# Every fourth row's dot product: a product on GpSimd and a sum on ScalarE in place of one operation on VectorE

## The reference

```python
eidx = jnp.take_along_axis(cidx, pos, axis=-1)      # 8 heads x 16 experts for each token
g = jax.nn.softmax(top_s, axis=-1)
u_sel = jnp.take(u, eidx, axis=0)                   # rows of 1024 numbers
a = jax.nn.gelu(jnp.einsum('chkd,cd->chk', u_sel, xc), approximate=False)
w = (g * a).astype(x.dtype)
v_sel = jnp.take(v, eidx, axis=0)
return jnp.einsum('chk,chkd->cd', w, v_sel)
```

## Time and profile before

| | |
|---|---|
| median of 3 runs | 2847.54 us (2843.93 to 2849.05) |
| the profiled execution | 2847.81 us, its span 2846.0 us |
| PE busy | 2144.6 us (75%) |
| DVE busy | 1585.1 us (56%) |
| ACT busy | 832.7 us (29%) |
| POOL busy | 749.6 us (26%) |
| all dot products (L1551) | 479.5 us in ring buffers, 158.3 us in arena buffers, x512 |
| all gathers issued (L2705) | x384 and x128, 545.30 MB with the queue's other transfers |

### The profile page before, as it was taken

The page is one execution under the profiler, slowest core; times in us unless marked ns, Lnnn a source line. Parts: engine busy times, 40 slices in busy tenths (PEclk is TensorE's granted clock), DMA queues, the critical chain, the costliest instruction groups (busy, mean ns, idle before and its releaser), DMA issues.

```text
span 2846.0 us, 33622 instructions
## 1 busy us (share of the span) xinstructions
PE 2144.6 (75%) x11828; PEld 1079.6 (38%) x11828; DVE 1585.1 (56%) x3312; ACT 832.7 (29%) x2340; POOL 749.6 (26%) x675
## 2 busy tenths in 40 slices
PE   6886767767567683776666667598987878988897
PEld 3552332222012262343332223276875443333332
DVE  5268648578446528856889877646555242222222
ACT  2215333433333312433343444323221111111111
POOL 1113434334335012334454445211111000000000
PEclk9888877778669786888998898899998889999999
DMA  7588999989999615899999899802111369999994
GB/s 274 213 339 314 408 422 405 422 339 393 422 421 412 239 67 212 327 422 406 416 396 397 329 421 415 359 33 88 58 45 63 119 281 415 420 420 419 417 419 186
DMA packets 122690, 894.55 MB, mean 314 GB/s; under 512 B 16400, under 2 KB 16912, under 8 KB 21776
## 3 DMA queue, kind: packets, MB, share of 16 engines
q0 software_dynamic: 77760, 545.30, 47.1%
q1 hardware_dynamic: 44752, 347.01, 30.1%
HBM read 893.82 MB, written 4.72 MB: 316 GB/s over the span
## 4 chain that ended last, share of the span: by engine, by line
PE 40%; DVE 27%; DMA 24%; ACT 4%; issue 3%; POOL 1%; SPq 0%; DVEq 0%; PEldq 0%; ACTq 0%; POOLq 0%
PE ps L155 39%; DMA ring<-in_peer_uv,idx_u 15%; DVE ring L1551 7%; DVE arena L76 5%; DMA ring<-in_w_gu 4%; ACT arena L125 3%; DMA arena<-in_peer_uv,idx_u 2%; DVE arena L1551 2%; DVE iu L113 2%; DVE arena L109 2%; PE ps L158 1%; DVE arena L97 1%; DVE small L93 1%; DMA arena<-in_w_gu 1%; DVE arena L118 1%
## 5 line engine op out<-in xcount | busy, mean ns | idle before, releaser
L155 PE MATMUL ps<-ring,arena 64*64 64x512 f32 (+3 forms) x4512 | 843.6, 715 | 339.4 <-ACT arena L125 293.0
L155 PE MATMUL ps<-arena 128*128 128x128 f32 (+8 forms) x3496 | 653.1, 501 | 196.8 <-ACT arena L125 160.3
L1551 DVE CUSTOM_DVE_ANT_0 ring<-ring,h 128x1024 f32<-128x1024 f32 x384 | 479.5, 1249 | 258.4 <-DMA ring<-in_peer_uv,idx_u 223.6
L2705 POOL DMA_INDIRECT ring<-in_peer_uv,idx_u x384 | 428.9, 1117 | 516.7 <-PE ps L155 477.3
L155 PEld LDWEIGHTS ps<-ring,arena 64*64 64x64 f32 (+3 forms) x4512 | 211.3, 149 | 841.3 <-ACT arena L125 578.1
L125 ACT ACTIVATE arena<-arena 128x1 f32<-128x1 f32 (+2 forms) x1051 | 270.8, 258 | 841.6 <-DVE arena L1551 739.7
L155 PEld LDWEIGHTS ps<-arena 128*128 128x128 f32 (+4 forms) x3496 | 323.3, 175 | 480.2 <-ACT arena L125 273.9
L125 ACT ACTIVATE arena<-ps 128x512 f32<-128x512 f32 (+2 forms) x222 | 122.7, 553 | 773.4 <-PE ps L155 702.5
L76 DVE TENSOR_TENSOR arena<-arena,ps 128x512 f32<-128x512 f32 (+1 forms) x154 | 90.9, 591 | 391.4 <-ACT arena L125 312.2
L155 PE MATMUL ps<-ring,hT 128*128 128x512 f32 (+2 forms) x832 | 281.2, 496 | 4.7 <-ACT hT L125 2.4
L2705 POOL DMA_INDIRECT arena<-in_peer_uv,idx_u x128 | 145.4, 1136 | 335.3 <-PE ps L155 259.5
(11 more groups left out here) (128 smaller groups left out, 1509.8 us busy)
## 6 DMA issues: line engine op xcount, KB each, us to landing
ring<-in_w_gu SPq DMA_DIRECT2D x98, 1024.0 KB, 22.5
ring<-in_w_down SPq DMA_DIRECT2D x52, 1024.0 KB, 22.6
ring<-in_peer_wq SPq DMA_DIRECT2D x16, 2048.0 KB, 11.3
arena<-in_w_gu SPq DMA_DIRECT2D x30, 1024.0 KB, 22.3
ring<-in_w_in SPq DMA_DIRECT2D x10, 2048.0 KB, 18.5
ring<-in_w_mod SPq DMA_DIRECT2D x16, 1024.0 KB, 7.3
arena<-in_w_in SPq DMA_DIRECT2D x6, 2048.0 KB, 11.8
ring<-in_w_o SPq DMA_DIRECT2D x6, 2048.0 KB, 8.2
```

The source lines that it names most:

```text
L155: return self.e.matmul(o, lhsT, rhs, start=start, stop=stop, skip_group_check=True)
L1551: v.done(v.e.tensor_tensor_reduce(out=row, in0=row, in1=h[:, n // 128, :], scale=1.0, scalar=0.0, op0=ALU.mult, op1=ALU.add, accum_out=aa[ ...
L2705: g.e.indirect_dma_start(out=landing(l, n), out_offset=None, in_=d["peer_uv"], in_offset=bass.IndirectOffsetOnAxis(ap=idx_u[:, n:n + 1], a ...
```

## The change

For the rows 3, 7, 11 to 255 of each layer VectorE skips `dots(n)`. GpSimd multiplies the row in place with `h`, after it has issued the gather six rows ahead. ScalarE then copies the product onto itself with an accumulated sum into the column of `aa`, before the gelu. All other rows stay as they were.

```diff
+DOTS_ASIDE, ASIDE_AT = range(3, 256, 4), 6
...
                 for n in range(256):
-                    dots(n)
+                    if n not in DOTS_ASIDE:
+                        dots(n)
...
                     w = aa[:, n:n + 1]
-                    a.wait_ge(*at("dots", l, n))
+                    if n in DOTS_ASIDE:
+                        row = landing(l, n)[:, 0:D]
+                        a.wait_ge(*at("product", l, n))
+                        a.act(row, row, ACT.Copy, accum_out=w)
+                    else:
+                        a.wait_ge(*at("dots", l, n))
                     a.act(w, w, ACT.Gelu)
...
-                for n in range(256 + 5):
+                def product(n):
+
+                    row = landing(l, n)[:, 0:D]
+                    g.wait_ge(*at("landed", l, n))
+                    g.tt(row, row, h[:, n // 128, :], ALU.mult, ("product", l, n))
+
+                for n in range(256 + ASIDE_AT):
                     if n < 256:
                         gather(n)
+                    if n - ASIDE_AT in DOTS_ASIDE:
+                        product(n - ASIDE_AT)
```

## The result

The changed kernel took 3112.93 us (median of 4 runs, 3107.73 to 3117.53) against 2848.3 us before on the same chip: ratio 1.0925, interval 1.0911 to 1.0939. That is 264.6 us slower. The direction was forecast, but the time lies 204 us above the forecast 2909 us and 128 us above the upper end of the range, 2985 us. The profiled execution has a span of 3108.3 us.

What follows compares the result with a forecast made beforehand. Row arrival by DMA was taken to bound the gather stages mostly, VectorE only in parts. Terms 20 + 26 - 18 + 37 - 9 + 5 = 61 us on 2847.81 us gave about 2909 us, range 2852 to 2985 us.

Steps and rivals of the forecast that it cites:

- The ring: Through GpSimd's queue, ScalarE and TensorE: a four-row cycle can't be shorter than 5.9 + 3W us.
- W: TensorE's weighted sum of one row, interpolated from the granted clock at 1.23 to 1.54 us.
- Rival D: Few rows in buffers, so products wait for landing and no loop forms; 2852 us, chance 0.11 shared with B.
- B: Rival: buffers and slack absorb the latency, the port takes back VectorE's saving; 2852 us, chance 0.11 with Rival D.
- Its fixed part: Gather, product, hand-over, ScalarE's sum and small operations, release to GpSimd: 5.88 us per four-row cycle, without weighted sums.
- So half is exposed: TensorE's other work, 0.9 to 4.2 us a cycle: half hidden before the moved row, half lengthening the cycle.
- Which cycles pay: Settled stretches: plus 20 and 26 us; mixed ones: plus 37 where DMA holds, minus 9 where VectorE does.
- the queue's slack: About 9 us by which gathers may issue late in each of two settled stretches, credited as minus 18 us.
- VectorE's relief: 128 dot products removed, 168 us of work, on the path only where VectorE is the limit.
- rival A: VectorE is the limit wherever the DMA share is below 1, so faster: about 2803 us, chance 0.10.
- rival C: At the VectorE-GpSimd port products nearly always get in first, VectorE losing 2.25 us for 1.31 saved: 2958 us, chance 0.15.
- Ends: Last row of each layer, with nothing behind to hide it: 1.31 us becomes 3.6, plus 5 us together.

Runs made afterwards that it cites:

- e1: Changed kernel with GpSimd's product five gathers ahead in its queue instead of six: 2918.17 us, ratio 1.0231.
- e9: Changed kernel with GpSimd zero fills in place of the product, still six gathers ahead, ScalarE still waiting and summing: 3102.09 us, ratio 1.0888.
- e6: Changed kernel with the 29 background pieces of the second chunk's attention moved away from the rows behind the product: 3074.30 us, ratio 1.0793.
- e10: Changed kernel with GpSimd zero fills in place of the product, four gathers ahead instead of six: 2849.37 us, ratio 1.0001.
- e3: Changed kernel with every fourth row's product on VectorE instead of GpSimd, the sum still on ScalarE: 2865.09 us, ratio 1.0052.
- e5: Kernel before, all dot products on VectorE, plus three GpSimd zero fills per used row that no other engine needs: 2877.07 us, ratio 1.0102.
- e4: Kernel before, all dot products on VectorE, plus GpSimd products whose output is not used: 2948.22 us, ratio 1.0349.

## Why the prediction was right in direction and wrong in size

**The ring: right.** "A cycle can't be shorter than 5.9 + 3W" was the mechanism. e1 shows it (one place is worth 1.52 us a cycle) and e9 shows that it is nearly all of the loss. Rival D is refuted by the 11.9 us that the products waited for their rows, and B by the time.

**Its fixed part: right.** The sum of gather, product, hand-over, ScalarE's part and the 0.31 was 5.88 us, 6.38 with the 0.5 us added for port and background; measured 1.12 + 2.42 + 0.20 + 2.23 + 0.31 = 6.28. The product was put at 2.25 and took 2.35 (median) to 2.42 us (mean); twice the 512-column row, 2.54, and the carried-on step, 2.03, held it between them.

**W: mis-sized.** I took it from the mean granted clock of a stretch, 1.41 us on average. By the eight matmuls of each row, W of the rows moved is 1.77 us (1.32 before), of the next two 1.61 and 1.34: 4.7 instead of 4.2 us a cycle. TensorE is kept from its next weighted sum for 4.6 us on average before row r (5.29 us idle below), and 74% of these rows then take over 1.8 us, near the 1.98 us at 1.2 GHz; before it was 23%.

**"So half is exposed": the step that failed.** Besides fixed part and W the cycle has 13.69 - 6.28 - 4.7 = 2.7 us; the prediction had 1.15 (half of TensorE's other busy time over the cycles). That is 1.5 of the 1.9 us by which its cycle of 11.8 us was short; W is 0.5. Taken from the start and end of every weighted sum, the 2.7 us are these: 1.9 us between the weighted sums of r, r + 1 and r + 2; 0.6 in front of gather r + 10, which starts that much later than the 0.31 us behind its weighted sum; and 0.1 in front of row r's. In the gaps between these weighted sums TensorE works on pieces for 1.7 us a cycle and is idle for 0.5 (where there is no gap the records overlap a little, so the net is 1.9).

So about half of TensorE's other work was exposed, as assumed. But this work was 3.1 us a cycle and not 2.3. Measured row by row it was 2.9 in the kernel before already: I had subtracted an interpolated 4W from the busy time of a stretch, and the rest came out too small. And neither TensorE's idle time inside the exposed pieces nor the late gather had a term. A usual place, timeline of 228 to 262 us:

```profile
235.77 1.99 PE L155 MATMUL ps<-ring,arena 64*64 64x512 f32 x8 [0.26 <-ACT arena L125]
...
237.69 2.19 PE L158 MATMUL ps<-cst,arena 128*128 128x128 f32 x16
...
239.81 1.95 PE L155 MATMUL ps<-arena 64*64 64x512 f32 x16
```

The weighted sum of r + 1 starts 4.0 us after row r's, and TensorE's own piece (L158) fills the 2 us between them. In 12 of 126 cycles TensorE is idle for over 2 us in these gaps. One of the dearest, timeline of 1928 to 1941 us, lines of other work left out:

```profile
1929.13 2.65 POOL L134 TENSOR_TENSOR ring<-ring,h 128x1024 f32<-128x1024 f32 x1
...
1934.01 1.98 PE L155 MATMUL ps<-ring,arena 64*64 64x512 f32 x8 [5.29 <-ACT arena L125]
1934.03 1.28 ACT L125 ACT_TABLE_LOAD   x1
1935.33 0.63 ACT L125 ACTIVATE arena<-arena 128x512 f32<-128x512 f32 x1
...
1935.99 1.57 ACT L125 ACTIVATE ring<-ps,small 128x128 f32<-128x128 f32 x4
...
1938.41 1.28 ACT L125 ACT_TABLE_LOAD   x1
...
1939.70 0.53 ACT L125 ACTIVATE arena<-arena 128x1 f32<-128x1 f32 x2
...
1940.72 1.98 PE L155 MATMUL ps<-arena 64*64 64x512 f32 x8 [4.73 <-ACT arena L125]
```

The dot product of row r + 1 had been done since 1929.6 us, yet its weighted sum starts 6.7 us after row r's: ScalarE does 5.7 us of background, two table loads in it, before it comes to r + 1, and TensorE stands idle 4.73 us. Gather r + 9 and product r + 4 come as much later. e6 moved pieces to where row r is waited for anyway and got 39 us back. The cycles without pieces on TensorE, rows 174 to 221 of the first layer, have a mean of 11.50 us, and 11.5 was forecast for that stretch; that is luck, since W was 0.9 us a cycle too short there and the exposed work, of which there was none, 0.5 too long. The same rows of the second layer, with pieces, took 12.86 us against 11.1.

**Which cycles pay: wrong, but the number did not come from it.** Floor and chain were compared with VectorE as the limit of half the mixed cycles (term -9) and the queue's slack as a one-time credit (-18). The ring holds in every stretch (the DMA share is at most 0.90), and a loss that returns each cycle uses 9 us of slack up within a few. But with the prediction's own chain in every stretch in which it is longer than the cycle before, the sum is 29 x 0.2 + 20.6 x 1.0 + 27.1 x 0.1 + 22 x 1.2 = 55 us, and its terms 20 + 26 - 18 + 37 - 9 gave 56. The miss is the length of the cycle: 13.47 us by the spans of the gathers against 11.8, over 127.5 cycles about 210 us, near the missing 204. One reading of the floor was off as well: the sixth stretch comes to 9.65 us and not 9.9; no term of the sum uses it.

**VectorE's relief: no net gain.** 168 us of dot products went away. The forecast was that VectorE's busy time falls, by less than that; it was 1586.4 us, against 1585.1 before. 119 us came back as blocked time of the other dot products: 384 x 1.245 = 478 us became 398.5 + 198.9 = 597. The other 50 came back in VectorE's remaining work, 35 of them in its TENSOR_TENSOR and SCALAR_TENSOR_TENSOR operations; the 58 of the form arena<-arena,small 128x512 took 0.89 us instead of 0.72. Where nothing is blocked (e10, VectorE busy for 1442.2 us) the kernel isn't faster either. The times refute rival A's 2803 us. That VectorE, at 85% in 1290 to 1600 us, set no part of the time there is not shown: e10 also has ScalarE's 1.25 us of latency, which cost 16 us in e3, and GpSimd's time in front of the gathers, which cost up to 28 us in e5, so a gain of that order could be hidden in it. One hint is that rows 62 to 90, where VectorE has the searches, took 166 us in e10's trace instead of 172 over both layers; single executions differ by more than these 6 us.

**The port, rival C: real, but not at its price here.** Each product blocks VectorE for 0.93 us on average, and it costs 12 to about 20 us inside the ring, where VectorE's time lies beside it, 39 once the ring is opened and about 71 with all dot products on VectorE (e4). By the Trainium skill ("SBUF — State Buffer", Who interferes with whom) it is GpSimd's reading of SBUF that contends; e4 and e5, where a product and a fill differ by 1.2 us of blocked VectorE for each, agree.

**Ends: right.** 3.6 us were expected from the start of the last product of a layer to the end of its sum. At the end of the first layer:

```profile
1054.21 2.35 POOL L134 TENSOR_TENSOR ring<-ring,h 128x1024 f32<-128x1024 f32 x1 [3.54 <-DMA ring<-in_peer_uv,idx_u]
...
1056.60 1.06 ACT L125 ACTIVATE ring<-ring 128x1024 f32<-128x1024 f32 x1 [0.55 <-POOL ring L134]
...
1057.78 0.53 ACT L125 ACTIVATE arena<-arena 128x1 f32<-128x1 f32 x2
```

1057.78 - 1054.21 = 3.57 us, against the 1.31 us of a dot product and its read the earlier trace rows, which ended the layer before.

**The range.** Its upper end let W rise on 60 cycles only, and had no case in which the pieces count with their waits. An upper bound with all of TensorE's other work exposed, 2.3 us more on the mean cycle instead of 1.15, would have been wider.

## What to carry to other kernels

An operation that is put into an in-order queue behind a transfer that waits for a buffer closes a ring through everything that frees the buffer. Write the ring down, count how many rows of it run in parallel, and charge its length to every turn: with background work between its steps that work counts in full, with its own waits, and every place earlier in the queue takes one step out. Before work is moved off an engine that looks busy, ask whether its relief shows in the end at all; here the same relief with the ring opened and the port left alone (e10), less what the new path itself costs, changed the time by 0.01%.

## What was not expected of the hardware

- A dot product whose record has begun is stretched by a GpSimd product that starts after it. Timeline of the changed kernel:

```profile
1041.06 3.78 DVE L1552 CUSTOM_DVE_ANT_0 ring<-ring,h 128x1024 f32<-128x1024 f32 x1
...
1041.39 2.35 POOL L134 TENSOR_TENSOR ring<-ring,h 128x1024 f32<-128x1024 f32 x1
```

The dot product starts 0.33 us earlier by its record, lasts 3.78 us instead of 1.23, and ends 1.1 us after the product, which took its usual 2.35 us. Nine more dot products of this trace, with records that begin 0.2 to 0.45 us before a product's, do the same (3.65 to 3.91 us). In the earlier trace rows the one that started second waited. Whether it had really begun, or its record starts before its first access, the trace doesn't say.

- A gather right behind a product took 1.49 us on GpSimd on average, over 1.5 us in 73 of 124 cases (2.03 at 821.02 above); the other gathers took 1.08. The long ones are not new: in the kernel before, without such products, 74 of 512 took over 1.5 us, up to 1.98. What makes a gather long is not shown.
- GpSimd wrote 1024 columns of zeros in 0.96 us, and VectorE's dot products beside it kept their 1.25 us (e5).
- TensorE's clock made the stall dearer: the weighted sum behind a wait of several microseconds took over 1.8 us in 74% of the moved rows; the rows two and three behind them have a median of 1.09 us. Both are read from the eight matmuls of each row, over all 128 cycles.
